# The remainder of the dense V rows computed on VectorE, between the gate products, in place of GpSimd

## The reference, cut to what matters

```python
a = jnp.einsum('thkd,td->thk', u_tab[eidx], hb)          # 128 experts chosen for each token
w = gelu(a) * gw
return jnp.einsum('thk,thkd->td', w, v_tab[eidx])
```

## Time and profile before

| | |
|---|---|
| median of 3 runs | 5751.99 us (5744.75 to 5753.68) |
| profiled execution | 5736.15 us, its span 5734.3 us |
| stage in layer 0 | from about 2218 us to 3100 us of the span |
| stage in layer 1 | from about 5015 us to 5700 us |
| busy over the span | PE 84%, DVE 70%, ACT 37%, POOL 41% |
| granted TensorE clock | 0.929 of full speed, mean |

### The profile page before, as it was taken

One profiled execution on the slowest core, in us unless ns is written; L12 is line 12 of the kernel. 1 busy time (PEld: TensorE's weight loads), 2 busy tenths in 40 slices (PEclk: granted clock), 3 DMA queues, 4 the chain that ended last, 5 costly groups with the idle time before them and its releaser, 6 DMA issues. The chain is left out here.

```text
span 5734.3 us, 72971 instructions
## 1 busy us (share of the span) xinstructions
PE 4832.2 (84%) x27874; PEld 4064.5 (71%) x27874; DVE 4022.5 (70%) x6929; ACT 2138.3 (37%) x3263; POOL 2372.2 (41%) x1488
## 2 busy tenths in 40 slices
PE   6975888899999997888886875777888999978887
PEld 5844876778888885666665543335788998978887
DVE  3146753199888874999997247983388774089997
ACT  2124222155555553222222144442355555522222
POOL 0001320056554664777772002440165553366663
PEclk8988988999999998999998887888899999989998
DMA  4111012267776897999994001112376675398884
GB/s 153 55 61 63 5 30 74 105 230 258 254 235 226 299 319 276 316 322 313 323 319 138 32 1 43 48 41 81 129 258 235 228 249 182 118 318 283 283 283 160
DMA packets 487495, 1052.48 MB, mean 184 GB/s; under 512 B 44758, under 2 KB 261580, under 8 KB 480492
## 3 DMA queue, kind: packets, MB, share of 16 engines
q1 hardware_dynamic: 372112, 636.63, 32.7%
q0 software_dynamic: 110592, 402.70, 20.6%
q10 hardware_dynamic: 4444, 8.48, 0.4%
HBM read 911.36 MB, written 136.31 MB: 183 GB/s over the span
## 5 line engine op out<-in xcount | busy, mean ns | idle before, releaser
L1522 POOL TENSOR_TENSOR u_lo<-u_raw,u_hi 128x1024 fp32r<-128x1024 f32 x256 | 630.5, 2463 | 1361.9 <-ACT u_hi L1627 1361.6
L1953 PE MATMUL banks<-w_hi,v_hi 128*128 128x512 f32 (+1 forms) x2048 | 778.8, 380 | 235.7 <-DVE w_lo L1979 173.4
L1570 PE MATMUL banks<-h_hi,ut_hi 128*128 128x512 f32 (+1 forms) x2048 | 796.6, 389 | 0.0
L1914 POOL TENSOR_TENSOR v_lo<-v_raw,v_hi 128x1024 fp32r<-128x1024 f32 x256 | 613.5, 2397 | 359.7 <-ACT v_hi L1930 358.0
L1953 PE MATMUL banks<-w_lo,v_hi 128*128 128x512 f32 (+1 forms) x2048 | 758.9, 371 | 0.0
L1570 PE MATMUL banks<-h_lo,ut_hi 128*128 128x512 f32 (+1 forms) x2048 | 758.6, 370 | 0.0
L1953 PE MATMUL banks<-w_hi,v_lo 128*128 128x512 f32 (+1 forms) x2048 | 758.2, 370 | 0.0
L1570 PE MATMUL banks<-h_hi,ut_lo 128*128 128x512 f32 (+1 forms) x2048 | 757.7, 370 | 0.0
L1953 PEld LDWEIGHTS banks<-w_hi,v_hi 128*128 128x128 f32 x2048 | 395.3, 193 | 344.3 <-POOL v_lo L1914 149.7
L1824 DVE CUSTOM_DVE_ANT_0 rows<-rows,banks 128x1024 f32<-128x1024 f32 x384 | 462.4, 1211 | 96.9 <-DMA rows<-peer_u,expert 80.4
L1905 POOL DMA_INDIRECT v_fetched<-peer_v,expert x384 | 427.5, 1113 | 142.7 <-DVE banks L2003 80.8
(11 more groups left out here) (415 smaller groups left out, 9715.5 us busy)
## 6 DMA issues: line engine op xcount, KB each, us to landing
u_raw<-peer_u SPq DMA_DIRECT2D x256, 512.0 KB, 5.3
v_raw<-peer_v SPq DMA_DIRECT2D x256, 512.0 KB, 5.3
gate_table<-part SPq DMA_DIRECT2D x28, 2048.0 KB, 8.4
activations<-acts SPq DMA_DIRECT2D x128, 256.0 KB, 4.2
acts_in<-activations SPq DMA_DIRECT2D x128, 256.0 KB, 4.4
gates<-gate_table SPq DMA_DIRECT2D x32, 1024.0 KB, 11.6
activations<-acts SPq DMA_DIRECT2D x128, 192.0 KB, 2.3
acts_in<-activations SPq DMA_DIRECT2D x128, 192.0 KB, 4.2
```

The source lines that it names most:

```text
L1522: nc.gpsimd.tensor_tensor(u_lo[:, i % 2], u_raw[:, i % 2], u_hi[:, i % 2].bitcast(F32), ALU.subtract)\
L1570: last = nc.tensor.matmul(out, u[:, i % 2, k * P:(k + 1) * P], h[:, k, 0:ND], start=(k == 0 and u is ut_hi and h is hi), stop=(k == DK - 1 ...
L1914: nc.gpsimd.tensor_tensor(v_lo[:, i % 2, r], v_raw[:, r], v_hi[:, i % 2, r].bitcast(F32), ALU.subtract)\
L1953: last = nc.tensor.matmul(out, v[:, i % 2, r, m * P:(m + 1) * P], w[:, i % 2, r], start=(r == 0 and v is v_hi and w is w_hi), stop=(r == G ...
```

## The change

The subtraction that makes `v_lo` leaves GpSimd, with its wait, and is put on VectorE as `remainder(j)`, directly behind `multiply(j)`. GpSimd's loop then only issues the fetches. The operands, the buffers and the semaphores stay the same.

```diff
@@ GpSimd
             s = 0
             for j in range(KEYS):
-                i, r = divmod(j, GROUP)
-                pool.wait_ge(v_hi_ready, j + 1)
-                nc.gpsimd.tensor_tensor(v_lo[:, i % 2, r], v_raw[:, r], v_hi[:, i % 2, r].bitcast(F32), ALU.subtract)\
-                    .then_inc(v_lo_ready, 1)
                 while s < plan.rows and s < (j - 3) * PER // GROUP + RING - 2:
                     fetch(s)
                     s += 1
@@ VectorE
+            def remainder(j):
+                i, r = divmod(j, GROUP)
+                dve.wait_ge(v_hi_ready, j + 1)
+                nc.vector.tensor_tensor(v_lo[:, i % 2, r], v_raw[:, r], v_hi[:, i % 2, r].bitcast(F32), ALU.subtract)\
+                    .then_inc(v_lo_ready, 1)
+
             for r in range(GROUP):
                 multiply(r)
+                remainder(r)
             for r in range(GROUP):
                 low(r)
@@ VectorE, loop over the groups i and blocks m
                         if m < GROUP:
                             multiply((i + 1) * GROUP + m)
+                            remainder((i + 1) * GROUP + m)
                         else:
                             low((i + 1) * GROUP + m - GROUP)
```

## The result

The changed kernel takes 5600.09 us (median of 4 runs, 5585.53 to 5602.60) against 5750.32 us before. The ratio is 0.9734, 95% interval 0.9716 to 0.9753: 150 us less, where 127 were forecast. On a second chip the same kernel took 5588.51 us, ratio 0.9711 (0.9695 to 0.9728). The profiled execution has a span of 5600.3 us.

The account below looks back on a forecast made before the run. VectorE, with no idle time, was taken to bound the kernel. 31 x (26.37 - 24.8) + 31 x (20.40 - 17.7) - 6 = 127 us off 5751.99 gave 5625 us, range 5575 to 5695 us.

Parts of the forecast that it names:

- What goes: Mix stages: GpSimd's subtraction no longer holds VectorE's products with two SBUF inputs, saving 6.77 and 7.72 us a group.
- What comes: VectorE in the mix stages: four subtractions of 1024 numbers a group, 1.15 us each, adding 4.60 us.
- What is next, transfers: DMA in the mix stages: about 350 GB/s taken as full rate, so periods of 24.8 and 17.7 us, not 24.2 and 17.28.
- The lower bound of 1.07: Least start-to-start cost in us of one 1024-number subtraction on VectorE, from twice 0.61 less the fixed part.
- The rival with DMA full: 319 GB/s is the cap: layer 0 gains nothing, layer 1 goes to 18.1 us a group; 5687 us, chance 0.15.
- The figure of 358 GB/s: HBM rate to one core by the Trainium skill; layer 0 would need 23.5 us a group, under VectorE's 24.2.
- The start: Start of each mix stage: the first 8 fetches go out beside v_raw, gates and x_t, costing 3 us a layer.
- The added wait: VectorE's remainder of tile 0 waits for v_hi: costs nothing, with 1.3 us spare in layer 1, over 3 in layer 0.
- TensorE and the cast in layer 1: Rival: they set layer 1's pace, each group 1 us longer if the cast comes 2.3 us later; 5656 us, chance 0.07.
- The lock stays: Rival: GpSimd's fetch work goes on holding VectorE's products, so the remainders are pure addition; 6037 us, chance 0.05.
- The trace agrees with the exception: GpSimd's fetches are not lengthened by VectorE's tensor_tensor: the fetch at 2611.12 began under a product and took 1.14 us.

Follow-up runs that it names:

- still_busy: The changed kernel, with GpSimd still doing one subtraction per expert tile on the identity matrix into a spare tile: 5768.11 us, ratio 1.0032.
- twice_2: The changed kernel with the remainder computed twice on VectorE, the first time into a tile nobody reads: 5865.64 us, ratio 1.0195.
- left_out: The changed kernel with no remainder subtraction anywhere, TensorE taking v_hi in place of v_lo: 5502.60 us, ratio 0.9572.
- pairs_again: The kernel before, VectorE's products set in pairs and GpSimd's subtraction released by a pair's end, rerun beside the changed kernel: 5490.48 us, ratio 0.9547.
- paced: The changed kernel, with GpSimd waiting before the fetches of tile j until v_lo of tile j is made: 5585.98 us, ratio 0.9721.

## Why the prediction was right, and where it was not

*What goes.* This was right, and it is shown from both sides: no product is held in the changed kernel, and held ones come back when GpSimd subtracts spare data. The 6.77 and 7.72 us a group were read as a difference, which was sound. That they were a property of the phase I had not seen; a sum of four times 2.4 us would have been wrong, as the expectation for *still_busy* was.

*What comes.* This was right too: four remainders are 24.18 - 19.60 = 4.58 us of a group, 1.15 us each, as forecast. *twice_2* gives 1.14. The lower bound of 1.07 was miscounted: by the slope in the prediction the fixed part is 0.61 - 4 x 0.14 = 0.05 us, so it is 2 x 0.61 - 0.05 = 1.17. Nothing hung on it.

*What is next, transfers.* Here a term of the sum was wrong in size. "I take 24.8 us (339 GB/s) instead of 24.2 in layer 0 and 17.7 (327 GB/s) instead of 17.28 in layer 1": the terms cost 31 x 0.6 + 31 x 0.4 = 31 us and measured zero. The windows at 359 GB/s were the demand of that moment, not a limit: *left_out* and *pairs_again* hold 385 and 386 GB/s for 550 us. Without these terms the forecast would have been 5594 us, where 5600 and, on the second chip, 5588.5 were measured. The periods alone gave 166 us; the medians show 150 us on the first chip and 167 us on the second, and why the first shows less than its periods isn't settled beyond the stages outside the change. The rival with DMA full fell with it.

*The figure of 358 GB/s* from the Trainium skill ("SBUF — State Buffer", "SBUF: two separate sides") does not hold here as a ceiling: the same transfers at 385 GB/s, mostly reads from HBM, speak against it. The measurement decides.

*The start.* The forecast was 3 us lost in each layer. Layer 0 reaches group 1 at 40.8 us in both kernels; layer 1 reaches it at 38.1 us, where it took 35.1 before. *paced* shows that the free fetches do cost 3.3 us in layer 0 as well (40.8 against 37.5 us). There the rest of the change gives back as much, which the forecast did not count.

*The added wait* costs nothing: VectorE has no idle time before `remainder` in any stretch of the steady state. *TensorE and the cast in layer 1* did not set the pace either, though TensorE at 99% shows how near it was.

*The lock stays* was wrong, as the changed kernel shows. But one sentence of the working failed, that on the other direction: "The trace agrees with the exception" of the Trainium skill ("SBUF — State Buffer", "Who interferes with whom"), so that fetches would not be lengthened by products. That section takes `tensor_tensor` out of the instructions that keep GpSimd from writing descriptors. This is GpSimd and then VectorE in layer 0 of the changed kernel:

```profile
2589.59 2.27 POOL L1905 DMA_INDIRECT v_fetched<-peer_v,expert  x1 [1.32 <-DVE banks L1999]
```

```profile
2589.23 0.69 DVE L1968 TENSOR_TENSOR acts_in<-acts_in,gates 128x512 f32<-128x512 f32 x1
2589.84 1.22 DVE L2006 TENSOR_TENSOR v_lo<-v_raw,v_hi 128x1024 fp32r<-128x1024 f32 x1
```

The fetches of the changed kernel take 1595 ns in the mean, up to 2277; before it was 1113 in the mean and 1234 at most. All 168 fetches longer than 1.25 us in the steady state of the two layers overlap a remainder, and with two remainders in a row (*twice_2*) a fetch takes up to 3.42 us. In *left_out*, which has no remainder, the mean is 1101 ns in layer 0. So a product of 1.2 us with two inputs does keep GpSimd's fetch waiting, and the measurement decides against the exception as I read it. Whether the fetch waits to read its row numbers from SBUF or to write its descriptors isn't shown. The row that I relied on showed it too, in small: the fetch at 2611.12 took 1.14 us, but fetches that meet no product take 0.93 to 0.95 us (35 of them in *left_out*), and those that begin 0.4 us into a short product take 1.13 at the median. It is harmless, as forecast: GpSimd is busy 387.90 us of 700, which is 13.4 us a group where 13.7 was the estimate, and the ring of 8 rows covers it.

## What to carry to other kernels

Before moving an instruction from one of two engines that hold each other up, compare start times on both: if the held instructions begin at the same distances from the other engine's in group after group, the size of the hold may be a matter of phase, and reordering may gain more than moving the work (here it ended 98 us below the changed kernel on the same chip). A single wait is no safe way to set the phase; count everything that stands between two instructions of the other engine. A transfer rate seen while an engine is the bound is that engine's demand; it is no limit until a kernel without the engine's work has been run. And a bare sum of start-to-start distances on an engine with no idle time forecast these periods to 0.04 us, closer than the allowances that I added to it.

## What the runs showed of the hardware that I had not expected

A GpSimd instruction with one SBUF input (128x1024, recorded at 2.80 us) held VectorE's two-input products for only the first 1.05 us; one with two inputs (2.40 us, or 1.91 us in *still_busy*) held them to its end; a memset of 0.97 us did not hold them at all. In the other direction, VectorE's 1.2 us product with two inputs lengthened indirect DMA instructions on GpSimd from at most 1.23 us to as much as 2.28 us, and even a 0.68 us product lengthened them from 0.94 to 1.13 us. And DMA moved 386 GB/s over 550 us in a mix of 4 KB, 2 KB and 512-byte pieces.
